# Gate matmuls in pairs at every second block of the u table, with ScalarE one step further ahead

## The reference, cut to what matters

```
q = h2 @ wq;  scores = q . keys            # 8 heads, 2 halves, 128 keys each
eidx, gates = top 16 of the sums of the top 16 x top 16 pairs, softmax
act = gelu(h2 . u_tab[eidx]);  w = gates * act
out = x + sum over the 8*16 experts of w * v_tab[eidx]
```

## Time and profile before

| | us |
|---|---|
| median of 3 runs | 1457.38 |
| lowest and highest of the runs | 1457.32, 1458.14 |
| the profiled execution | 1456.08 |
| its span, first to last instruction | 1454.4 |
| PE busy | 1432.2 (98%) |
| DVE busy | 1162.5 (80%) |
| ACT busy | 699.1 (48%) |

### The profile page before, as it was taken

The page is one execution under the profiler, slowest core; times in us unless marked ns, Lnnn a source line. Parts: engine busy times, 40 slices in busy tenths (PEclk is TensorE's granted clock), DMA queues, the critical chain, the costliest instruction groups (busy, mean ns, idle before and its releaser), DMA issues.

```text
span 1454.4 us, 23527 instructions
## 1 busy us (share of the span) xinstructions
PE 1432.2 (98%) x7901; PEld 1247.9 (86%) x7901; DVE 1162.5 (80%) x2215; ACT 699.1 (48%) x1238; POOL 324.0 (22%) x300
## 2 busy tenths in 40 slices
PE   8999989999999999999999999999999999999998
PEld 5878756599999999999999999888888888888887
DVE  6555573989989999999999953797778788888885
ACT  5454672133469734995459833443333333333331
POOL 1000200034023202332124521343222222322210
PEclk9999999999999999999999999999999999999999
DMA  8120304068579986899779999899999999999993
GB/s 304 45 73 1 145 13 162 1 237 290 201 245 354 404 291 221 280 391 385 242 259 369 417 411 359 297 360 366 346 337 344 339 338 354 343 371 345 361 344 144
DMA packets 175764, 403.04 MB, mean 277 GB/s; under 512 B 14672, under 2 KB 96592, under 8 KB 175184
## 3 DMA queue, kind: packets, MB, share of 16 engines
q1 hardware_dynamic: 138832, 268.02, 50.8%
q0 software_dynamic: 36864, 134.23, 25.4%
HBM read 347.67 MB, written 54.53 MB: 277 GB/s over the span
## 4 chain that ended last, share of the span: by engine, by line
PE 89%; DVE 5%; DMA 3%; ACT 1%; issue 1%; SPq 0%; DVEq 0%; ACTq 0%
PE psum L540 52%; PE psum L1108 36%; DMA uraw<-in_uT 3%; DVE sco L1905 0%; DMA acts_scratch<-act_s 0%; DVE x L1717 0%; DVE itop L1909 0%; DVE itop L1903 0%; DMA wring<-in_chunks 0%; DVE pr L1745 0%; DVE mstat L1752 0%; DVE top L1901 0%; DVE top L1907 0%; ACT pr L1296 0%; DVE x L1809 0%
## 5 line engine op out<-in xcount | busy, mean ns | idle before, releaser
L540 PE MATMUL psum<-hhi,uhi 128*128 128x384 f32 x1024 | 348.3, 340 | 3.5 <-ACT act_s L1452 3.4
L540 PE MATMUL psum<-hlo,uhi 128*128 128x384 f32 x1024 | 342.6, 335 | 0.0
L1531 ACT ACTIVATE vhi<-vraw 128x1024 fp32r<-128x1024 f32 x128 | 135.9, 1061 | 319.6 <-PE psum L1108 313.7
L515 POOL DMA_INDIRECT urow<-in_u,eidx x128 | 164.1, 1282 | 505.8 <-DVE urow L1845 356.2
L1108 PE MATMUL psum<-vhi,whi 128*128 128x512 f32 x768 | 236.5, 389 | 0.0
L1108 PE MATMUL psum<-vlo,whi 128*128 128x512 f32 x768 | 236.5, 389 | 0.0
L1108 PE MATMUL psum<-vhi,wlo 128*128 128x512 f32 x768 | 236.5, 389 | 0.0
L515 POOL DMA_INDIRECT urow<-in_v,eidx x120 | 135.1, 1126 | 384.0 <-DVE acc L2065 383.4
L2059 DVE TENSOR_TENSOR vlo<-vraw,vhi 128x1024 fp32r<-128x1024 f32 x128 | 156.6, 1223 | 72.6 <-ACT vhi L1531 71.9
L540 PE MATMUL psum<-hhi,ulo 128*128 128x384 f32 x1024 | 198.3, 334 | 0.0
L540 PEld LDWEIGHTS psum<-hhi,uhi 128*128 128x128 f32 x1024 | 192.2, 188 | 5.1 <-ACT uhi L1445 4.3
(11 more groups left out here) (302 smaller groups left out, 1784.9 us busy)
## 6 DMA issues: line engine op xcount, KB each, us to landing
uraw<-in_uT SPq DMA_DIRECT2D x128, 512.0 KB
vraw<-in_v SPq DMA_DIRECT2D x128, 512.0 KB
acts_scratch<-act_s SPq DMA_DIRECT2D x128, 192.0 KB
gates_scratch<-stage SPq DMA_DIRECT2D x48, 512.0 KB
gring<-gates_scratch SPq DMA_DIRECT2D x32, 768.0 KB
aring<-acts_scratch SPq DMA_DIRECT2D x128, 192.0 KB
wring<-in_chunks SPq DMA_DIRECT2D x18, 512.0 KB, 4.8
wout<-in_wout SPq DMA_DIRECT2D x1, 4096.0 KB, 12.6
```

The lines of the kernel that those rows point to most:

```text
L515: g.indirect_dma_start(urow[k], None, table, bass.IndirectOffsetOnAxis(eidx[:, n % HK:n % HK + 1], 0)).then_inc(row_in[k], 16)
L540: return nc.tensor.matmul(out, lhsT, rhs, start=start, stop=stop, skip_group_check=shared)
L1531: a_(vhi[:, k, :], vraw[:, k, :], ACT.Copy).then_inc(s["vhi_ready"], 1)
```

## The change

TensorE runs gate step 0 before block h, then steps 1 and 2 one after the other before blocks h+1 and h+2, steps 3 and 4 before blocks h+3 and h+4, and so on; step 15 stands alone before block h+15. ScalarE stages step n at turn h+n, after the activations of block h+n-1 (it was step n-1, ahead of the activations), and weighs step n+2 at the end of that turn (it was n+1). VectorE makes the one-hots of step n+2 at turn n (it was n+1), and those of steps 0 and 1 before its first turn. SyncE's program is not touched.

```diff
@@ TensorE
-                with pe.Fori(h // 4, h // 4 + 4) as q:
-                    for k in range(4):
+                def gate_steps(q, last):
+
+                    up(0, 4 * q)
+                    for k in (1, 3):
                         gates(t - 1, q, k)
+                        if not (last and k == 3):
+                            gates(t - 1, q, k + 1)
                         up(k, 4 * q + k)
+                        if k == 1:
+                            up(2, 4 * q + 2)
+                gates(t - 1, h // 4, 0)
+                with pe.Fori(h // 4, h // 4 + 3) as q:
+                    gate_steps(q, False)
+                gate_steps(h // 4 + 3, True)
@@ ScalarE
                 for tt in range(DT):
-                    n = i - HOT_AT[tt]
-                    if 0 < n <= 16:
-                        stage_gates(16 * tt + n - 1)
+                    if i == HOT_AT[tt]:
+                        weigh(16 * tt + 1)
                 if i:
                     activations(i - 1)
                 for tt in range(DT):
                     n = i - HOT_AT[tt]
-                    if -1 < n + 1 < 16:
-                        weigh(16 * tt + n + 1)
+                    if 0 <= n < 16:
+                        stage_gates(16 * tt + n)
+                    if n == -1 or 0 <= n < 14:
+                        weigh(16 * tt + (0 if n == -1 else n + 2))
@@ VectorE
                 one_hot(0)
+                one_hot(1)
                 for n in range(16):
                     up_to(HOT_AT[tt] + n + 1, 0)
-                    if n < 15:
-                        one_hot(n + 1)
+                    if n < 14:
+                        one_hot(n + 2)
                     up_to(0, dotted[0] + (2 if tt == DT - 1 else 1 + n % 2))
```

## The result

| | before | after |
|---|---|---|
| median us (4 runs each) | 1457.41 | 1475.42 |
| lowest and highest | 1457.32, 1458.14 | 1473.76, 1477.04 |
| profiled execution, its span | 1456.08, 1454.4 | 1473.76, 1472.0 |

The ratio is 1.0121, 95% interval 1.0108 to 1.0134. So the change costs 18 us, where 8 were forecast: the sign is right, and the time is just outside the range (1457.5 to 1474.0).

What follows compares the result with a forecast made beforehand. TensorE, busy for 98% of the span, was taken to bound the kernel. From the profiled 1456.1, - 1.8 (seams) + 9.8 (stalls for stored gates) = 1464.1 us; the runs' median lies 1.3 above, so 1465.4; range 1457.5 to 1474.

Steps and rivals of the forecast that it cites:

- the seams: TensorE going from one kind of matmul to the other and back: 21 fewer at 0.086 us, 1.8 us gained.
- L - 6.2: TensorE's stall in us at steps 10 and 14; L is the time from the gate store's issue to its landing.
- the first places: Staging of step 8 in each tile, waiting for the first chunk's part 3: stalls 2.0, 1.3, 3.6, together 6.9 us.
- the second places: Staging of step 12 in each tile, waiting for the second chunk's part 3: 8.1 us by formula, a third taken, 2.7.
- the prediction's 3.2 us for 512 KB: Skill-page estimate for one store (about 2.0 us plus bytes over 436 GB/s); by it only the seams' gain would be left.
- VectorE ... I cost it at nothing.: VectorE loses its lead of a step and falls back 1.5 us in a tile; costed at nothing, without cover +1.5.
- The 0.5 us a place: Added stall at each of six places because the u block's load now goes out just ahead of the store; 3 us.
- the term 3.6 + 0.5: Third tile's first place: stall of 3.6 us by the formula, plus 0.5 for the load ahead of the store.
- The second place: Third tile, staging of step 12: 5.5 us by the formula, a third of it taken, plus 0.5 for the load.
- The 1.6 us of give-back: Part of the third tile's stalls returned as TensorE's idle time behind it shrinks; 1.6 us taken off.
- Loads. I take nothing: Loads of u blocks for a pair's second block: late by nothing to 3 us a pair, costed at nothing.
- late loads and VectorE as well: Rival: in the third tile late loads and VectorE's lag add 9 us on top, 1474 us; chance 0.14.

Runs made afterwards that it cites:

- run 2: The changed kernel with each part of staged gates stored one block earlier, nothing else; ratio 1.0013 to the kernel before.
- run 10: The changed kernel with VectorE lowering a block further ahead and staged gates stored a block earlier; 1457.12 us, ratio 0.9992 to the kernel before.
- run 7: The changed kernel with 24 instead of 32 dots woven into the third tile, the other 8 after it; 1471.35 us, ratio 1.0086.
- run 9: The changed kernel with VectorE lowering a block further ahead inside the gate stretches; 1464.88 us, ratio 1.0036.
- run 11: The changed kernel with SyncE issuing a turn's stores ahead of the load of its u block; 1475.89 us, ratio 1.0110.
- run 6: The kernel before with VectorE alone making one-hots two steps ahead, TensorE's and ScalarE's orders as before; ratio 1.0044.
- run 1: The changed kernel with TensorE's order of before (one gate step, one block), ScalarE's and VectorE's new orders kept; 1466.07 us, ratio 1.0048.
- run 3: The changed kernel with the pairs on even steps (0 and 1, 2 and 3, ...), stores as in the changed kernel; ratio 1.0120.
- run 8: The changed kernel with staged gates stored a block earlier and 24 dots in the third tile; 1460.30 us, ratio 1.0013.
- run 5: The kernel before, unchanged, profiled again beside the others; one run, 1458.61 us.

## Why the prediction was wrong

**Right: the seams.** 21 at 0.086 were forecast as 1.8 us; tiles without a gap show 0.70 us a tile, 2.1 in all (runs 2 and 10).

**Right: the place and the formula of the stall.** Gaps stand before steps 10 and 14 and nowhere else in the tiles. With L = 8.9 and 8.5 "L - 6.2" gives 2.7 and 2.3 us at the first places of tiles 1 and 2; the gaps are 2.63 and 2.13. At the second places L = 6.9 and 7.3 gives 0.7 and 1.1, the gaps are 0.50 and 0.92. With the measured time of the store's issue in place of 1.5, the formula meets the gap before step 10 to within 0.15 us in all three tiles of the changed kernel and of runs 7, 9 and 11. The forecast for tiles 1 and 2, stalls and seams together, was 5.0 us; they lost 5.4. Run 2 removes them by moving the stores alone, so this cause is shown. That the sum came out so near is in part luck: the first places were forecast too short (2.5 and 1.8 us), and at the second ones a third of the formula stood for a guess (0.9 each).

**The page's price for one transfer.** The Trainium skill (DMA: Bandwidth & Descriptors, section "Anatomy of one DMA — SWDGE (gpsimd) path") fits its price to transfers that GpSimd issues, so the prediction's 3.2 us for 512 KB, an estimate by that page, is not what the page says of SyncE's stores. The waits in the changed kernel ended 6.9 to 12.6 us after the issue. No run here shows such a store in an empty queue.

**Wrong: "VectorE ... I cost it at nothing."** This is the step that failed. The prediction saw that VectorE's lead of a step was gone and looked only at whether `hotLo` and `ulo` were still in time for TensorE. They were. But SyncE waits for the same lowering before it issues a turn's load, and the stores of that turn stand behind the load. In tile 3, where VectorE also falls back by its own work, this held the store itself: it left 2.9 us after block h+6 (802.01 against 799.07, where step 7 starts) instead of 1.5, 0.96 us after the lowering had ended. ScalarE's activations ahead of it had ended at 800.80, 0.6 us later than in tile 1; the other 0.7 us of the delay against tile 1 are the wait for the lowering. In all tiles the lowering sets the load's place in the queue. The 0.5 us a place for that were too little: with the lead back, L is 1.9, 0.4 and 1.6 us shorter at the first places (run 9). Run 6 prices VectorE's part alone at 6 us, with neither of the other two parts there; run 9 gives back the lead and saves 11 to 12 us of the changed kernel's 18. The parts do not add up: 6 us for VectorE's order alone and 16 us that go with the stores' place are more than 18. Both act on ScalarE's one wait for the store.

**Wrong in size: the first place of tile 3**, the term 3.6 + 0.5. It measured 7.68 us. L was taken from before (9.8, plus 0.5 for the new order of the queue) and was 12.6, and the store left 1.4 us later than assumed. With both, 2.9 + 12.6 + 3.4 - 11.15 = 7.8: the formula holds, its inputs did not. No term stood for the clock, which took 2.6 us more behind this gap. The second place, forecast as a third of 5.5 and 0.5 more, had no gap at all: its store had landed within 5.2 us. The 1.6 us of give-back never came; the blocks behind took 1.7 us more. In sum, tile 3 and the blocks behind it were forecast at 3.0 us and cost 10.3.

**"Loads. I take nothing"** held for TensorE. ScalarE did wait longer for loads, but between the tiles, where the blocks last as before. The rival "late loads and VectorE as well" (1474) came nearest the time, but not by its own mechanism: of its signs, gaps at every pair are nowhere, waits on `uraw` inside the stretches are absent in tiles 1 and 2 and come to 4.9 us in tile 3, whose one gap stands behind the wait for stored gates, and no `hotA` or `hotLo` ends last before a gap. Its nearness is in good part luck.

**Wrong in the experiments: room counted at one place.** Runs 1 and 3 show that ScalarE, with 0.5 us free in a step, carries a wait of 5 us on to steps further back. The pair's second step and the turns after it must be in the sum too.

**Not settled.** Of the 18 us, 2.0 lie ahead of all gate work, 1.6 of them across the trunk's window with the clock at 0.76. This fall stands in the profiles of the changed kernel and of nine of the ten variants (not in run 7), and in neither of the two profiles of the kernel before. The code there is the same; why the clock falls, and whether the change has a part in it, is open. Why L reaches 12.6 in tile 3 was tried with fewer rows gathered (8.5 at that place in run 7); how much of it is the rows' own traffic and how much VectorE's time for the dots was not separated.

## What to carry to other kernels

When an engine's work is moved a step earlier, list every wait that hangs on that engine, down to who issues the next DMA. Here VectorE's lost lead cost nothing at the engine it feeds and 6 us through the queue. A wait on an engine that is 90% busy is not covered by room at the next consumer: the engine stays late until its little free time has worked the wait off. Where the reuse of a buffer waits for a store, and the reuse is moved earlier, move the issue of the store along with it.

## What the runs showed of the hardware

Where ScalarE waited for it, a store of 512 KB took 5.8 (run 11) to 12.6 us (the changed kernel) from issue to the end of the wait, with the DMA engines at a share of 0.9 to 1.03 in the windows shown. In stretches with the same instructions L differed by 1 us and more from one profile to another (runs 2 and 8).

The clock can't be read off the length of a gap alone. A gap of 7.68 us on TensorE was followed by a granted clock of 0.50, gaps of 4.7 and 3.2 us by 0.56 and 0.57 over 4 us (run 9), one of 3.2 us by 0.50 (run 3), and gaps of 2.4 us (run 2) and 2.1 us (run 5, the kernel before) by 0.50 as well. Gaps of 2.63 and 2.13 us in the first two tiles of the changed kernel were not followed by a fall. In the trunk of the changed kernel the clock fell with TensorE 95% busy (6.65 of 7 us).

Putting two groups of 16 f16 matmuls of 128 columns one behind the other, rather than with 24 matmuls of 384 columns between them, saved 0.10 us each time (runs 2 and 10).
